# Order of two pieces in each slot of TensorE's queue: attention piece ahead of the hgrn2 level

## The chip, the cores and the metric

The kernel runs on one core of one Trainium2 chip. The metric is the device time of one execution in microseconds (us); lower is better. The time given for the kernel before is the median of 3 runs.

## What is computed

The program is a network of one dense block and two further layers over 256 tokens of width 1024. In each of the two layers (called layer 0 and layer 1 here, `l` in the code) the normed tokens `h` are projected once and the result feeds two token mixers, a gate for each, and then a mixture of experts:

```python
proj = h @ w_in
hq, hf, hi, hgate, cq, ckv, kr, gates = jnp.split(proj, IN_SPLITS, axis=-1)
o_a = hgrn2_mix(...)                      # 4 heads of 128, chunks of 64 tokens
o_a = rmsnorm(o_a, ...) * silu(hgate)
y_a = o_a @ w_br_a
y_b = mla_mix(cq, ckv, kr, pos, ...) @ w_br_b
g = sigmoid(gates)
merged = g_a * y_a + g_b * y_b
return merged @ w_out
```

`hgrn2_mix` is a linear recurrence with a decay per channel. Within a chunk it needs attention-like products of q and k, weighted by exp of differences of a running sum. `mla_mix` is a latent attention of 8 heads: q and k of 96 numbers per head (64 plain, 32 rotated), scores with a mask by chunks, a softmax, and the product with v of 64 numbers per head.

## The kernel before

Each engine has a queue of its own, written out by hand; semaphores join them. Weights come through a ring of 6 tiles of 1 MB in SBUF (`RING = 6`). The DMA of a tile (queue of SyncE, L432) waits until the tile six places earlier has been used by TensorE (`tiles_used`).

The products that must be exact to float32 are made of three: each such weight tile is split by ScalarE into a high part (`split` in its queue, L632, two halves) and by VectorE into the rest (`split` in its queue, L1808, two halves, event `mix_lo`).

The change is in the stretch that both layers have behind the projections: eight slots n = 0 to 7. TensorE does in slot n of the kernel before:

1. `by_token(gates{n})` (L1075): 48 matmuls of 256 columns for a tile of the gates, into bank n % 3. From slot 2 on it waits for the split of its tile, which ScalarE and VectorE make in their slot n - 2; from slot 3 on for the read of the bank (`gates`).
2. In layer 0 alone: three `ada` tiles (L1333, 48 matmuls of 32 rows by 256 columns), the modulation of layer 1.
3. The hgrn2 level n (L1579): 8 matmuls of 128 by 128 (16 passes in the trace) into banks 4 and 5. It waits for `hy` (written by VectorE in its slot n - 1) and `level_added`; its end is the event `level`.
4. `mla(n)`: a piece of the latent attention into banks 6 and 7. Slots 0 and 1 turn q, slots 2 and 3 turn k (`mla_turn`, L1519), slots 4, 5 and 6 make scores (`mla_scores` 0, 1 and 2, L1527), slot 7 turns the first block's probabilities (L1559). Slots 1 to 4 wait for ScalarE's copy of the turned piece before (`qT_out`, `kT_out`), slots 5 and 6 for the row maxima of the scores before (`mla_max`), slot 7 for `mla_max` and `mla_p`.

Behind the eight slots stand level 8 (L1588, waits for the eighth `hy`), the turns of the second block's probabilities (L1533), the hgrn2 output (L1597 to L1600) and the attention's output (L1614, L1616).

VectorE does in slot n: the span of level n + 1 (L2276, L2280, or L2288 to L2292; event `scans`), then it takes level n from its banks (`add_level`: L2303 in slot 0, L2305 in the others; it waits for `level`), multiplies the decays into `hy` (L2324, L2325; waits for `decay`), splits a gates tile (slots 0 to 5), in slots 4 to 6 masks the scores (L2334 or L2340; waits for `mla_s`) and takes their maximum (L1992, L1993; event `mla_max`), and in slots 5 to 7 scales the probabilities of the piece before (L2349, L2351; event `mla_p`).

ScalarE does in slot n: tanh of the gates (L948), the two exps of the decays (L959, L960; it waits for `scans` and for `hy` of VectorE's slot n - 1), its split of a gates tile (slots 0 to 5; in layer 0 it waits for the tile's DMA), then the copy of the turned q or k (L966, L972) in slots 0 to 3, or the exps of the scores (L979; waits for `mla_max`) in slots 4 to 6.

Of the kernel before, what the change touches and what calls it, by code (L numbers as in the profile page):

```python
# [67 lines left out]
def build(nc, a):  # L68

    ctx = ExitStack()  # L70
    with ctx:
# [293 lines left out]
        def slot_view(pos, kind):  # L365
            w = ring[:, pos % RING, :]
            if kind == 3 * QL:
                return w[:, 0:3 * QL].rearrange("p (k n) -> p k n", k=3)
            if kind in (512, 1024):
                return w.rearrange("p (k n) -> p k n", n=kind)  # L370
            return w[:, 0:KC * kind].rearrange("p (k n) -> p k n", k=KC)
# [43 lines left out]
        def _(sp):  # L415
# [18 lines left out]
            for entry in stream:  # L434
# [4 lines left out]
                if len(entry) == 4:  # L439
                    _, gate, up, down = entry  # L440
                    half = lambda w, e, kh: w[:, e, 4 * kh:4 * kh + 4, :]
                    down_half = lambda e, kh: down[:, e, 2 * kh:2 * kh + 2, :]
                    load(pos + 0, half(up, 0, 0))
                    load(pos + 1, half(gate, 0, 0))
                    load(pos + 2, half(gate, 0, 1))
                    load(pos + 3, half(up, 0, 1))
                    with sp.Fori(0, NE - 1) as i:
                        load(pos + 4, half(up, i + 1, 0), i)
                        load(pos + 5, down_half(i, 0), i)
                        load(pos + 6, down_half(i, 1), i)  # L450
                        load(pos + 7, half(gate, i + 1, 0), i)
                        load(pos + 8, half(gate, i + 1, 1), i)
                        load(pos + 9, half(up, i + 1, 1), i)
                    load(pos + 6 * NE - 2, down_half(NE - 1, 0))
                    load(pos + 6 * NE - 1, down_half(NE - 1, 1))
                    continue
                _, n, gate, up, down = entry

                def step(i, c, first=False):
# [565 lines left out]
        def _(pe):  # L1025
            mm, tr = pe.matmul, pe.transpose

            def landed(pos, i=0):
                pe.wait_ge(ring_full[pos % RING], 16 * i + 16 * (pos // RING + 1))
# [38 lines left out]
            def by_token(name, out, x_lo):  # L1068

                w = mix_parts(name)  # L1070
                h_parts = (hT_hi, x_lo)
                for t in range(T):
                    for k in range(KC):
                        for m, (hp, wp) in enumerate(PARTS):
                            ins = mm(out[:, t * FB:(t + 1) * FB], h_parts[hp][:, k, t * P:(t + 1) * P], w[wp][:, k, :],  # L1075
                                     start=k == 0 and m == 0, stop=k == KC - 1 and m == 2)
                ins.then_inc(tiles_used, 1)
# [247 lines left out]
            def ada(l, m, out):  # L1325

                pos = place[f"ada{m}.{l}"]
                landed(pos)
                w = slot_view(pos, FB)
                row, half = m // 2, m % 2  # L1330
                for k in range(KC):
                    g = 32 * (k % 4)
                    ins = mm(out[g:g + 32, half * FB:(half + 1) * FB], cpick[:, 12 + 32 * k - row:44 + 32 * k - row], w[:, k, :],  # L1333
                             start=m == 0 and k < 4, stop=m >= ADA_SLABS - 2 and k >= 4, skip_group_check=True)
                ins.then_inc(tiles_used, 1)
# [140 lines left out]
            for l in range(LAYERS):  # L1476
# [39 lines left out]
                def mla_turn(half, src, event):  # L1516
                    for h in range(4 * half, 4 * half + 4):
                        for t in range(T):
                            ins = tr(T_BANK[h % 4 // 2][0:DQK, (h % 2) * SEQ + t * P:(h % 2) * SEQ + (t + 1) * P],  # L1519
                                     src[:, t, h, :], ident[:, :])  # L1520
                    ins.then_inc(s[event], 1)

                def mla_scores(part):
                    for h in (range(MH), range(4), range(4, MH))[part]:
                        t, keys = (1, SEQ) if part else (0, P)
                        at = (h % 4 if part else h) * keys
                        ins = mm(T_BANK[at // 512][:, at % 512:at % 512 + keys], qT96[0:DQK, h, t * P:(t + 1) * P],  # L1527
                                 kT96[h // 4][0:DQK, h % 4, 0:keys], start=True, stop=True)
                    ins.then_inc(s["mla_s"], 1)
# [7 lines left out]
                def mla(n):  # L1537

                    if n < 2:
                        if n:  # L1540
                            pe.wait_ge(s["qT_out"], 2 * l + 1)
                        mla_turn(n, q96, "mla_qT")
                    elif n < 4:
                        if n == 2:
                            pe.wait_ge(s["qT_out"], 2 * l + 2)
                        else:
                            pe.wait_ge(s["kT_out"], 2 * l + 1)
                        mla_turn(n - 2, k96, "mla_kT")
                    elif n < 7:
                        if n == 4:  # L1550
                            pe.wait_ge(s["kT_out"], 2 * l + 2)
                        else:
                            pe.wait_ge(s["mla_max"], 3 * l + n - 4)
                        mla_scores(n - 4)
                    else:
                        pe.wait_ge(s["mla_max"], 3 * l + 3)
                        pe.wait_ge(s["mla_p"], 3 * l + 1)
                        for h in range(MH):
                            ins = tr(T_BANK[h // 4][:, (h % 4) * P:(h % 4 + 1) * P], p_first[:, h, :], ident[:, :])  # L1559
                        ins.then_inc(s["mla_pT"], 1)  # L1560

                for n in range(8):
                    if n >= 3:
                        pe.wait_ge(s["gates"], 8 * l + n - 2)
                    by_token(f"gates{n}.{l}", bank[n % 3], hT_lo_l)
                    if l == 0:
                        for m in range(ADA_EACH[1] * n, ADA_EACH[1] * (n + 1)):
                            ada(1, m, bank[3])
                    if n == 0:
                        pe.wait_ge(s["hk"], run)  # L1570
                        pe.wait_ge(s["hq"], run)
                        left, right = hk, hq
                    else:
                        pe.wait_ge(s["hy"], 8 * l + n)
                        pe.wait_ge(s["level_added"], 9 * l + n)
                        left = right = hy[:, :].rearrange("p (h s) -> p h s", h=HGH)
                    for t in range(T):
                        for h in range(HGH):
                            ins = mm(bank[4 + t][:, h * P:(h + 1) * P], left[:, h, t * P:(t + 1) * P],  # L1579
                                     right[:, h, t * P:(t + 1) * P], start=True, stop=True)  # L1580
                    ins.then_inc(s["level"], 1)
                    mla(n)

                pe.wait_ge(s["hy"], 8 * l + 8)
                pe.wait_ge(s["level_added"], 9 * l + 8)
# [946 lines left out]
```

## Time and profile before

| what | us |
|---|---|
| median of 3 runs | 1886.56 (1885.85 to 1888.33) |
| time of the profiled execution | 1887.39 |
| its span, first to last instruction | 1885.7 |
| TensorE busy | 1693.9 (90%) |
| VectorE busy | 1184.9 (63%) |
| ScalarE busy | 975.0 (52%) |
| mean granted TensorE clock | 0.948 of full speed |
| eight slots of layer 0, first gates matmul to level 8 | 686.25 to 788.02 |
| eight slots of layer 1, first gates matmul to level 8 | 1347.92 to 1421.71 |

TensorE has the largest busy share; the page's share is an average over stages with different limits, so the stretch of the slots is read by itself. The time outside the span is 1.7 us.

### The profile page before, as it was taken

How to read it: one execution, taken by the hardware profiler on the slowest of the kernel's cores; microseconds unless marked ns; L12 is line 12 of the kernel's file. 1: busy time of each engine (PE TensorE's matmuls, PEld its weight loads, DVE VectorE, ACT ScalarE, POOL GpSimd, SP SyncE). 2: the span in 40 equal slices, each digit the busy share in tenths (PEclk: the TensorE clock that was granted, in tenths of full speed). 3: DMA queues.
4: the chain of work that ended last, by engine and by line, in shares of the span. 5: the costliest groups of instructions: out<-in, count | busy, mean ns of one | idle time of the engine just before them, and what ended most of it. 6: DMA issues, size and time to landing. Idle time of an engine off the chain costs nothing.

```text
span 1885.7 us, 26698 instructions
## 1 busy us (share of the span) xinstructions
PE 1693.9 (90%) x10028; PEld 1408.3 (75%) x10028; DVE 1184.9 (63%) x1669; ACT 975.0 (52%) x1365; POOL 26.7 (1%) x58
## 2 busy tenths in 40 slices
PE   6999897899996989886899999979898769999995
PEld 6999785499995968743688888869695357888884
DVE  5544355554447444723788888854574378888886
ACT  4444344154434423401788888744341049888883
POOL 2000000000000000001000000000000010000000
PEclk9999998999998989998799999989899969999998
DMA  8555478845552559722398998935332308898992
GB/s 255 191 188 178 154 244 279 272 156 190 178 190 88 169 169 348 267 89 89 113 335 314 333 329 319 331 110 166 125 112 89 112 32 297 316 332 325 324 335 76
DMA packets 245831, 401.83 MB, mean 213 GB/s; under 512 B 6522, under 2 KB 151596, under 8 KB 245756
## 3 DMA queue, kind: packets, MB, share of 16 engines
q1 hardware_dynamic: 244792, 398.77, 61.6%
q0 software_dynamic: 592, 0.93, 0.2%
q10 hardware_dynamic: 372, 1.07, 0.2%
q8 instruction: 54, 0.88, 0.2%
q14 instruction: 21, 0.17, 0.0%
HBM read 399.70 MB, written 1.05 MB: 213 GB/s over the span
## 4 chain that ended last, share of the span: by engine, by line
PE 82%; DVE 10%; ACT 4%; issue 2%; DMA 1%; ACTq 0%; DVEq 0%
PE bank L1226 19%; PE bank L1168 14%; PE bank L1250 9%; PE bank L1097 8%; PE bank L1075 8%; PE bank L1181 6%; PE bank L1063 4%; PE bank L1262 3%; PE bank L1333 2%; DMA sb_ring<-in_w_in 1%; PE bank L1508 1%; PE bank L1086 1%; PE bank L1579 1%; DVE sb_w_lo L1808 1%; DVE sb_w_lo L1873 1%
## 5 line engine op out<-in xcount | busy, mean ns | idle before, releaser
L1873 DVE TENSOR_TENSOR sb_w_lo<-sb_ring,sb_moe_hi 128x1024 fp32r<-128x1024 f32 x384 | 448.4, 1220 | 29.5 <-ACT sb_moe_hi L697 29.2
L697 ACT ACTIVATE sb_moe_hi<-sb_ring 128x1024 fp32r<-128x1024 f32 x384 | 381.5, 1056 | 69.8 <-PE bank L1250 33.7
L1829 DVE TENSOR_TENSOR sb_w_lo<-sb_ring,sb_w_hi 128x1024 fp32r<-128x1024 f32 x128 | 151.1, 1222 | 172.1 <-ACT sb_w_hi L652 172.1
L1168 PE MATMUL bank<-sb_hT_hi,sb_w_hi 128*128 128x256 f32 x704 | 200.6, 285 | 3.6 <-DVE sb_hT_lo L1785 3.6
L652 ACT ACTIVATE sb_w_hi<-sb_ring 128x1024 fp32r<-128x1024 f32 x128 | 128.4, 1051 | 144.6 <-PE bank L1168 131.1
L1168 PE MATMUL bank<-sb_hT_hi,sb_w_lo 128*128 128x256 f32 x704 | 200.4, 285 | 0.0
L1168 PE MATMUL bank<-sb_hT_lo,sb_w_hi 128*128 128x256 f32 x704 | 200.4, 285 | 0.0
L1226 PE MATMUL bank<-sb_moe_hi,sb_xw_hi 128*128 128x512 f32 x480 | 193.6, 403 | 0.0
L1226 PE MATMUL bank<-sb_w_lo,sb_xw_hi 128*128 128x512 f32 x480 | 190.9, 398 | 0.0
L1226 PE MATMUL bank<-sb_moe_hi,sb_xw_lo 128*128 128x512 f32 x480 | 190.2, 396 | 0.0
L1250 PE MATMUL bank<-sb_moe_hi,sb_hid_hi 128*128 128x512 f32 x512 | 145.4, 396 | 2.9 <-DVE sb_hid_hi L1899 2.9
L1808 DVE TENSOR_TENSOR sb_w_lo<-sb_ring,sb_proj_hi 128x1024 fp32r<-128x1024 f32 x76 | 89.5, 1221 | 92.1 <-ACT sb_proj_hi L632 92.0
L1168 PEld LDWEIGHTS bank<-sb_hT_hi,sb_w_hi 128*128 128x128 f32 x704 | 136.4, 194 | 4.6 <-DVE sb_w_lo L1817 3.9
L1168 PEld LDWEIGHTS bank<-sb_hT_lo,sb_w_hi 128*128 128x128 f32 x704 | 136.4, 194 | 0.7
L1168 PEld LDWEIGHTS bank<-sb_hT_hi,sb_w_lo 128*128 128x128 f32 x704 | 136.3, 194 | 0.0
L1075 PE MATMUL bank<-sb_w_lo,sb_hT_hi 128*128 128x256 f32 x480 | 136.1, 284 | 0.0
L632 ACT ACTIVATE sb_proj_hi<-sb_ring 128x1024 fp32r<-128x1024 f32 x76 | 76.4, 1056 | 105.6 <-PE bank L1063 43.2
L1075 PE MATMUL bank<-sb_proj_hi,sb_hT_hi 128*128 128x256 f32 x416 | 120.0, 289 | 4.8 <-ACT sb_arena L942 4.8
L1075 PE MATMUL bank<-sb_proj_hi,sb_hT_lo_l 128*128 128x256 f32 x416 | 117.9, 283 | 0.0
L1250 PEld LDWEIGHTS bank<-sb_moe_hi,sb_hid_hi 128*128 128x128 f32 x512 | 93.8, 188 | 21.4 <-DVE sb_hid_hi L1899 3.4
L1226 PEld LDWEIGHTS bank<-sb_moe_hi,sb_xw_lo 128*128 128x128 f32 x480 | 91.3, 190 | 21.6
L1226 PEld LDWEIGHTS bank<-sb_w_lo,sb_xw_hi 128*128 128x128 f32 x480 | 91.4, 190 | 20.0
(465 smaller groups left out, 3132.9 us busy)
## 6 DMA issues: line engine op xcount, KB each, us to landing
sb_ring<-in_w_up SPq DMA_DIRECT2D x64, 1024.0 KB, 5.3
sb_ring<-in_w_gate SPq DMA_DIRECT2D x64, 1024.0 KB, 5.3
sb_ring<-in_w_down SPq DMA_DIRECT2D x64, 1024.0 KB, 4.8
sb_ring<-in_ada_w SPq DMA_DIRECT2D x48, 1024.0 KB, 7.7
sb_ring<-in_w_in SPq DMA_DIRECT2D x46, 1024.0 KB, 5.3
sb_ring<-in_ffn_w_in SPq DMA_DIRECT2D x44, 1024.0 KB, 5.0
sb_ring<-in_ffn_w_out SPq DMA_DIRECT2D x22, 1024.0 KB, 4.9
sb_ring<-in_w_out SPq DMA_DIRECT2D x12, 1024.0 KB, 5.0
```

Of the source, the lines that this page charges most:

```text
L632: A(mix_hi(name)[:, c], ring[:, pos % RING, c], ACT.Copy).then_inc(s["mix_hi"], 1)
L652: A(w_hi[:, q % 2, c], ring[:, (pos0 + q) % RING, c], ACT.Copy).then_inc(s["w_hi"], 1)
L697: A(moe_hi[:, q % 3, c], ring[:, at % RING, c], ACT.Copy).then_inc(s["moe_hi"], 1)
L1075: ins = mm(out[:, t * FB:(t + 1) * FB], h_parts[hp][:, k, t * P:(t + 1) * P], w[wp][:, k, :], start=k == 0 and m == 0, stop=k == KC - 1 an ...
L1097: ins = mm(out[2 * t + half][:, :], lhs[:, kk, t * P:(t + 1) * P], w[:, kk, half * 512:(half + 1) * 512], start=start and kk == 0, stop=st ...
L1168: ins = mm(bank[4 + 2 * p + b][:, jj * SEQ:(jj + 1) * SEQ], w[wp][:, k, jj * P:(jj + 1) * P], h_parts[hp][:, k, :], start=k == 0 and m == ...
L1181: ins = mm(acc[2 * t + half][:, :], h, w[wp][:, kk, half * 512:(half + 1) * 512], start=start and kk == 0 and m == 0, stop=stop and kk == ...
L1226: ins = mm(out[:, :], x_parts[xp][:, 4 * kh + k, 0:P], w[wp][:, k, :], start=kh == 0 and k == 0 and m == 0, stop=kh == 1 and k == 3 and m ...
L1250: ins = mm(bank[6 + half][:, :], h[hp][:, 2 * kh + kk, :], w[wp][:, kk, half * 512:(half + 1) * 512], start=kh == 0 and kk == 0 and m == 0 ...
L1808: ins = tt(w_lo[:, pos % RING, c], ring[:, pos % RING, c], mix_hi(name)[:, c].bitcast(F32), ALU.subtract)
L1829: ins = tt(w_lo[:, slot, c], ring[:, slot, c], w_hi[:, q % 2, c].bitcast(F32), ALU.subtract)
L1873: ins = tt(w_lo[:, slot, c], ring[:, slot, c], moe_hi[:, q % 3, c].bitcast(F32), ALU.subtract)
```

## The change

In the loop over the slots the call of `mla(n)` moves from behind the level to ahead of it. Nothing is added or removed, and the queues of the other engines stay as they are, instruction for instruction.

```diff
                     if l == 0:
                         for m in range(ADA_EACH[1] * n, ADA_EACH[1] * (n + 1)):
                             ada(1, m, bank[3])
+                    mla(n)
                     if n == 0:
                         pe.wait_ge(s["hk"], run)
                         pe.wait_ge(s["hq"], run)
...
                             ins = mm(bank[4 + t][:, h * P:(h + 1) * P], left[:, h, t * P:(t + 1) * P],
                                      right[:, h, t * P:(t + 1) * P], start=True, stop=True)
                     ins.then_inc(s["level"], 1)
-                    mla(n)
```

On TensorE, layer 1, the end of slot 4 (L1579 the level, L1527 the scores of part 0) stood before as:

```order
L1579 MATMUL bank<-sb_arena 128x128 [waits level_added,hy]
L1579 MATMUL bank<-sb_arena 128x128 x7
L1527 MATMUL bank<-sb_small_a,sb_arena 128x128 [waits kT_out]
L1527 MATMUL bank<-sb_small_a,sb_arena 128x128 x3
L1527 MATMUL bank<-sb_small_b,sb_arena 128x128 x4
L1075 MATMUL bank<-sb_proj_hi,sb_hT_hi 128x256 [waits mix_lo,gates]
```

The same place stands now as follows (the level is L1580 in the changed file):

```order
L1527 MATMUL bank<-sb_small_a,sb_arena 128x128 [waits kT_out]
L1527 MATMUL bank<-sb_small_a,sb_arena 128x128 x3
L1527 MATMUL bank<-sb_small_b,sb_arena 128x128 x4
L1580 MATMUL bank<-sb_arena 128x128 [waits level_added,hy]
L1580 MATMUL bank<-sb_arena 128x128 x7
```

The eight score matmuls, with their wait, have moved ahead of the level; in slots 5 and 6 the wait that moves with them is that for `mla_max`.

On TensorE, layer 0, slot 5 with the ends of the `ada` matmuls (L1333) ahead of it, as a difference:

```order
 L1333 MATMUL bank<-sb_ring,sb_cpick 32x256 x24
-L1579 MATMUL bank<-sb_arena 128x128 x8
 L1527 MATMUL bank<-sb_small_a,sb_arena 128x256 x4
+L1580 MATMUL bank<-sb_arena 128x128 x8
 L1075 MATMUL bank<-sb_proj_hi,sb_hT_hi 128x256
```

The level now stands between the scores of part 1 and the next gates tile. The last slot of layer 0, with level 8 (L1588) behind it:

```order
 L1333 MATMUL bank<-sb_ring,sb_cpick 32x256 x24
-L1579 MATMUL bank<-sb_arena 128x128 x8
 L1559 MATMUL bank<-sb_ident,sb_arena 128x128 x8
+L1580 MATMUL bank<-sb_arena 128x128 x8
 L1588 MATMUL bank<-sb_arena 128x128 x4
 L1533 MATMUL bank<-sb_ident,sb_arena 128x128 x8
```

Level 7 now stands behind the eight turns of L1559 and directly ahead of level 8.

## Rows read from the trace of the kernel before

**Rows 1.** The page: span, and busy time of two engines.

```profile
span 1885.7 us, 26698 instructions
PE 1693.9 (90%) x10028; PEld 1408.3 (75%) x10028; DVE 1184.9 (63%) x1669; ACT 975.0 (52%) x1365; POOL 26.7 (1%) x58
```

**Rows 2.** Stretches of the slots: length, busy PE, PEld, DVE, ACT, POOL, clock, DMA.

```profile
690.00:790.00 100.00, 94.30 (x956) 81.25 (x955) 54.55 (x87) 37.33 (x79) 0.00 (x0) 0.98 1.00 327
1340.00:1440.00 100.00, 91.18 (x705) 83.84 (x704) 70.35 (x116) 45.59 (x95) 0.00 (x0) 0.98 0.32 106
```

**Rows 3.** Waits, 1345 to 1435 us: who waited for whom, us, times, longest.

```profile
DVE sb_arena L2305 <- PE bank L1579: 10.5, 5, 2.5
PE bank L1588 <- DVE sb_arena L2325: 3.1, 1, 3.1
```

**Rows 4.** Chain that ended last, layer 1: start us, us, what.

```profile
1356.60 5.75 PE bank L1075 x48
1362.35 1.79 PE bank L1579 x16
1364.14 0.87 PE bank L1519 x8
...
1387.59 1.80 PE bank L1579 x16
...
1396.93 0.18 DVE sb_stat L1993
...
1401.94 0.69 DVE sb_arena L2324
...
1408.00 0.17 DVE sb_stat L1993
...
1416.46 0.18 DVE sb_stat L1993
```

**Rows 5.** Timeline of DVE, layer 1: start, us, engine, line, [idle <- releaser].

```profile
1394.36 1.28 DVE L2334 TENSOR_TENSOR sb_arena<-bank,sb_mla_mask 128x512 f32<-128x512 f32 x2
...
1398.81 1.35 DVE L2305 COPY_PREDICATED sb_arena<-sb_level_mask,bank 128x512 f32<-128x512 int32 x2 [1.12 <-PE bank L1579]
...
1411.29 1.36 DVE L2305 COPY_PREDICATED sb_arena<-sb_level_mask,bank 128x512 f32<-128x512 int32 x2
...
1417.87 1.34 DVE L2305 COPY_PREDICATED sb_arena<-sb_level_mask,bank 128x512 f32<-128x512 int32 x2
...
1420.36 0.69 DVE L2324 TENSOR_TENSOR sb_arena<-sb_arena 128x512 f32<-128x512 f32 x1 [1.15 <-ACT sb_arena L960]
```

**Rows 6.** Timeline of ACT, layer 0: copy of the turned q.

```profile
706.55 1.06 ACT L966 ACTIVATE sb_arena<-bank 96x512 f32<-96x512 f32 x2
```

**Rows 7.** Timeline of PE, layer 0: slots 1 and 5, and level 8.

```profile
706.25 2.05 PE L1579 MATMUL bank<-sb_arena 128*128 128x128 f32 x16
...
754.29 2.05 PE L1579 MATMUL bank<-sb_arena 128*128 128x128 f32 x16
758.95 2.87 PE L1527 MATMUL bank<-sb_small_a,sb_arena 96*128 96x256 f32 x8 [2.60 <-DVE sb_stat L1993]
...
788.02 1.16 PE L1588 MATMUL bank<-sb_arena 128*128 128x128 f32 x8 [1.95 <-DVE sb_arena L2325]
```

**Rows 8.** Chain, layer 0: scores of part 2 (slot 6) and level 7.

```profile
773.00 1.73 PE bank L1527 x8
...
783.21 2.00 PE bank L1579 x16
```

**Rows 9.** Timeline of DVE, layer 0: level 7 taken from its banks.

```profile
785.30 1.34 DVE L2305 COPY_PREDICATED sb_arena<-sb_level_mask,bank 128x512 f32<-128x512 int32 x2 [4.63 <-PE bank L1579]
```

**Rows 10.** Clock behind the gap ahead of level 8, layer 1 (columns as rows 2).

```profile
1422.00:1425.50 3.50, 3.50 (x19) 3.50 (x19) 1.61 (x5) 0.31 (x1) 0.00 (x0) 0.51 0.00 0
```

**Rows 11.** Timeline of PE: L1635 behind equal gaps in layers 0 and 1.

```profile
832.99 1.09 PE L1635 MATMUL bank<-sb_ident,sb_arena 128*128 128x128 f32 x8 [2.71 <-DVE sb_arena L2394]
...
1466.43 1.95 PE L1635 MATMUL bank<-sb_ident,sb_arena 128*128 128x128 f32 x8 [2.71 <-DVE sb_arena L2394]
```

## Prediction

> **What bounds the kernel now.** The page comes first: TensorE is busy for 90% of the span and VectorE for 63% [rows 1]. The change touches only the eight slots of each layer, so I read those by windows. There TensorE is busy for 94% of the stretch in layer 0 and 91% in layer 1; the DMA engines are full in layer 0 and at a third in layer 1 [rows 2]. A reorder on a busy engine is free as long as nobody waits for the piece that comes later, so the next view is who waits for the level: VectorE (L2305) waits for L1579 five times in layer 1, 10.5 us in all, at most 2.5 us [rows 3]. These waits have different weight. The chain that ended last tells it. Through slots 0 to 3 of layer 1 it is all TensorE: gates 5.75, level 1.79, turn 0.87 us, slot after slot [rows 4]. From the level of slot 4, which starts at 1387.59, it leaves TensorE: VectorE and ScalarE carry it through L1993 at 1396.93, 1408.00 and 1416.46, until level 8 starts on TensorE at 1421.71 after an idle time of 3.1 us [rows 3, 4]. So from slot 4 on the level's end feeds the chain, and TensorE waits for that chain at its end. In layer 0 the DMA sets ScalarE's and VectorE's pace up to slot 5; then VectorE idles 4.63 us for level 7 [rows 9], and TensorE idles 1.95 us for what comes of it [rows 7]. Nobody waits for the scores or the turned pieces: in slot 4 of layer 1 VectorE comes to the scores at 1394.36 [rows 5], and they end at about 1387.59 + 1.80 + 1.73 = 1391.1 [rows 4, 8].
>
> **The change part by part.** The number of instructions does not change, nor what each costs: 8 turns are 0.87 us, 8 score heads 1.73, a level 1.79 in layer 1 and 2.0 in layer 0 [rows 4, 8]. What changes is that each level ends later by the length of the piece ahead of it, and that the piece's own wait now stands ahead of the level.
>
> Slots 0 to 3, layer 1: the level ends 0.87 us later. VectorE waits 2.35 us for each of levels 1 to 4 (10.5 less the 1.12 of slot 5, over four) [rows 3, 5], and what it makes next, `hy`, is not needed until the level of the next slot, a gates tile of 5.75 us later. The split that follows serves the gates tile two slots on. TensorE has no new wait: the total per slot stays 8.41. Cost 0; without that cover it would be 0.87 once.
>
> Slot 4, layer 1: scores 0 (1.73) now stand ahead of level 4. Level 4 ends at 1387.59 + 1.73 + 1.80 = 1391.12, not 1389.39. VectorE stood waiting there, so its chain starts 1.73 late, and the maximum of slot 4 (L1993) ends at 1398.83, not 1397.10.
>
> Slot 5, layer 1: the gates end at 1396.87 as before (1391.12 + 5.75). Before, the level went next and hid the wait for `mla_max`. Now TensorE idles until 1398.9, makes scores 1 until 1400.6 and level 5 until 1402.4. VectorE took level 5 at 1398.81 [rows 5]; now it does so at 1402.5, 3.7 late. It had spare time there, since `hy` waited for ScalarE until 1401.94 [rows 4]. ScalarE's part comes at 1401.94 + 1.73 = 1403.7, VectorE's own at 1402.5 + 1.35 = 1403.85. So `hy` is 1.9 late, and the second maximum ends at 1408.17 + 1.9 = 1410.07.
>
> Slot 6, layer 1: gates from 1402.4 to 1408.15, idle until 1410.1, scores 2 until 1411.8, level 6 until 1413.6. VectorE took level 6 without idle time at 1411.29 [rows 5]; now at 1413.7, 2.4 late. The third maximum ends at 1416.63 + 2.4 = 1419.05.
>
> Slot 7, layer 1: gates until 1419.35, L1559 until 1420.2, level 7 until 1422.0. VectorE takes it from 1422.1 to 1423.45, where it began at 1417.87 before. ScalarE's exps, behind the third maximum, come 2.4 late. So L2324 starts at about 1423.5, against 1420.36 [rows 5], and level 8 follows it: **+3.1 us** for layer 1.
>
> Layer 0, slots 0 to 4: slot 1 shows a new wait. TensorE reaches the piece at 706.25 [rows 7], but ScalarE's copy of the first turned q runs from 706.55 to 707.6 [rows 6]: 1.3 us idle, which the level hid. Such waits come back up to slot 4, as TensorE arrives 2 us ahead of each copy. They don't add up, because the copies stand at the pace of the DMA. TensorE is then one level, 1.98 us, behind its old place at each slot's end. Would later use of tiles starve the DMA? The engines are full, with tiles queued [rows 2]; a slip of 2 us in a cadence of 12 us for four tiles (levels 1 and 5 start 48.0 us apart [rows 7]) should stay inside that queue. Its cost is 0; were it not covered, it would be up to 2 us.
>
> Layer 0, slot 5: scores 1 start at 758.95 with or without the change, since their maximum hangs on VectorE's chain from the DMA. Before, level 5 (754.29 to 756.3) lay in the wait; 2.60 us idle were left [rows 7]. Now the whole wait is idle, and the level goes behind the scores: +1.98 on TensorE, and there is no later wait in slots 6 and 7 to take it back. In slot 7, L1559 adds its 0.87 ahead of the level. Level 7 ended at 783.21 + 2.00 [rows 8], and VectorE had long been waiting [rows 9]: it takes it 1.98 + 0.87 = 2.85 later, and level 8, which hangs on that alone, moves from 788.02 by **+2.85 us**.
>
> Sum of both layers: 3.1 + 2.85 = 5.95. Behind level 8 the same chain as before follows, on TensorE and VectorE, and nothing there waits for a transfer, so I give nothing back.
>
> One price is unsettled: TensorE's clock after a gap. After the 3.1 us gap ahead of level 8 of layer 1 [rows 3] the granted clock was 0.51 for 3.5 us, the 1.2 GHz level [rows 10]. The same code, L1635, behind a gap of 2.71 us in both layers, took 1.09 us in one and 1.95 in the other [rows 11]: a gap of this size costs sometimes 0 and sometimes some 0.9 to 1.7 (3.5 us at 0.51, if all of it is matmul). The change makes the gap before level 8 of layer 0 some 2.75 long instead of 1.95, and adds two of 1.9 to 2.0 in layer 1; the one of 1.95 was followed by 1.16 for L1588, so full speed [rows 7]. I charge half a drop of about 1 us: +0.5. At the other end, three drops would cost 5.1. The Trainium skill (TensorE: Matmul & The Clock Gate, part 1) says that an idle stretch halves the clock, and that the phase in which it is looked at varies from run to run; the rows on L1635 agree. By that rule the new gaps are a toss, and the sum would lie between the plain one and the one with all drops.
>
> Forecast: the profiled execution goes from 1887.39 (span 1885.7) to 1893.8 (span 1892.2), as 1.7 lie around the span. The median of before is 0.8 below its profiled time, so the median comes to 1886.56 + 5.95 + 0.5 = **1893.0**.
>
> **The rivals.**
> - *The order is neutral.* TensorE's work is the same, and 10.5 us of waiting for levels in layer 1 [rows 3] can swallow the delay. It does in slots 0 to 3. Against it: in slots 5, 6 and 7 VectorE idles 1.12 us, nothing and nothing before L2305 [rows 5]. It would give 1886.6. Chance 0.12.
> - *One layer alone pays.* If the DMA's pace, or a slack that I missed, takes back layer 0's part, 1886.6 + 3.1 = 1889.7 stays; with layer 1's part gone, 1889.4. For it: layer 0 runs at full DMA. Against it: VectorE's 4.63 us in slot 7 are for TensorE, not for a transfer [rows 9]. Chance 0.12.
> - *More clock drops.* Each of the longer gaps costs its 1.7: with two beside the sum 1886.6 + 5.95 + 3.4 = 1895.9, with three 1897.6. For it: rows 10. Against it: the gap of 1.95 that kept its speed. Chance 0.14.
> - *Faster: the attention pieces bind.* The scores reach VectorE earlier by a level, 1.79 or 2.0 us, in slots 4 to 6. If L2334 and L2340 waited for TensorE, each slot's chain would shorten by as much: at most 3 x 1.79 + 3 x 2.0 = 11.4, so 1875.2. It decides as soon as VectorE idles before L2334 for L1527. Against it: VectorE came to L2334 3.2 us after the scores of slot 4 and shows no idle time before it [rows 5]. Chance 0.03.
>
> **How the numbers follow.** The forecast as summed has 0.59. The range goes from one layer alone (1889.4) to the sum with between two and three drops (1896.6); neutral and faster, 0.15 together, lie outside, with a little at the top. About 0.2% (3.8 us, so 1890.3) is what a measurement can tell from no change. Slower beyond it: the forecast, the clock case and a share of the one-layer case, 0.76; same: neutral and the rest of one-layer, 0.20; faster 0.04.
>
> **What would show it.** In the new trace: TensorE idle before L1527 in slots 5 and 6 of layer 1, some 1.9 us each, for L1993; idle before L1519 in slots 1 to 4 of layer 0, for ScalarE's copies; level 8 some 76.9 us after the first gates matmul of layer 1 (73.8 before) and 104.6 in layer 0 (101.8 before); the experts as long as before. The prediction is wrong if VectorE's idle time in slots 5 to 7 does not move, if the DMA of layer 0 shows pauses that stretch the slots, or if the stretch behind level 8 gives the delay back.

## The result and the profile after

| | median us | range, runs |
|---|---|---|
| before | 1888.18 | 1885.85 to 1893.80, 7 |
| changed | 1900.64 | 1898.31 to 1907.47, 7 |

The changed kernel takes 1.0068 of the time of before, 95% interval 1.0054 to 1.0083: 12.8 us (10.2 to 15.7) slower. The forecast was 1893.0, the range ended at 1896.6. Later runs of the same kernel gave 1.0054 (1.0033 to 1.0075) and 1.0049 (1.0036 to 1.0062). Three executions far outside all others, one of the changed kernel (3014.90 us) and two of before (7167.72 and 2224.72), are left out everywhere.

The page of the changed kernel, against [rows 1]:

```profile
span 1898.3 us, 26698 instructions
PE 1699.3 (90%) x10028; PEld 1410.8 (74%) x10028; DVE 1185.8 (62%) x1669; ACT 974.7 (51%) x1365; POOL 26.7 (1%) x58
```

Instructions are the same; the span is 12.6 us longer and TensorE is busy for 5.4 us more, with the same matmuls.

The timeline of PE in layer 0 (start us, us, engine, line, op; idle time and who ended it), against [rows 7]. L1580 is the level, L1579 before:

```profile
706.09 1.08 PE L1519 MATMUL bank<-sb_ident,sb_arena 128*96 128x128 f32 x8 [1.39 <-ACT sb_arena L966]
707.00 1.95 PE L1580 MATMUL bank<-sb_arena 128*128 128x128 f32 x16
...
757.65 2.97 PE L1527 MATMUL bank<-sb_small_a,sb_arena 96*128 96x256 f32 x8 [2.72 <-DVE sb_stat L1993]
...
784.62 1.95 PE L1580 MATMUL bank<-sb_arena 128*128 128x128 f32 x16
789.39 2.07 PE L1588 MATMUL bank<-sb_arena 128*128 128x128 f32 x8 [2.82 <-DVE sb_arena L2325]
791.25 1.72 PE L1533 MATMUL bank<-sb_ident,sb_arena 128*128 128x128 f32 x8
```

The slots started at 684.71 here (686.25 before), so level 8 comes 104.68 us after them, where it was 101.77. The wait for ScalarE's copy is there (1.39, and 0.82 and 0.84 in slots 2 and 3; none in slot 4, where one was forecast), the wait for the maximum stands alone (2.72), and the gap ahead of level 8 grew from 1.95 to 2.82. Behind that gap L1588 and L1533 took 2.07 and 1.72 us; before, L1588 took 1.16 behind its shorter gap [rows 7]. The windows view (columns as in rows 2) has the granted clock there at 0.52 and then at 1.00:

```profile
789.40:792.80 3.40, 3.40 (x16) 3.40 (x17) 1.85 (x6) 0.00 (x0) 0.00 (x0) 0.52 1.02 406
792.80:796.00 3.20, 3.20 (x32) 3.20 (x30) 0.31 (x1) 2.37 (x3) 0.00 (x0) 1.00 0.03 10
```

PE in layer 1, slots started at 1353.16 (1347.92 before):

```profile
1404.18 2.00 PE L1527 MATMUL bank<-sb_small_a,sb_arena 96*128 96x256 f32 x8 [2.02 <-DVE sb_stat L1993]
1406.02 1.95 PE L1580 MATMUL bank<-sb_arena 128*128 128x128 f32 x16
1415.77 2.34 PE L1527 MATMUL bank<-sb_small_b,sb_arena 96*128 96x256 f32 x8 [2.06 <-DVE sb_stat L1993]
1417.90 3.29 PE L1580 MATMUL bank<-sb_arena 128*128 128x128 f32 x16
...
1427.65 1.95 PE L1580 MATMUL bank<-sb_arena 128*128 128x128 f32 x16
1432.43 1.16 PE L1588 MATMUL bank<-sb_arena 128*128 128x128 f32 x8 [2.83 <-DVE sb_arena L2325]
```

Level 8 comes after 79.27 us, against 73.79. The two new waits are 2.02 and 2.06 long. Behind the first the next pieces ran at full clock (level 5: 1.95); behind the second they did not (level 6: 3.29). VectorE's timeline shows the releaser turned round: it idles for each of levels 5, 6 and 7, where it idled 1.12 us, none and none [rows 5]:

```profile
1408.07 1.39 DVE L2305 COPY_PREDICATED sb_arena<-sb_level_mask,bank 128x512 f32<-128x512 int32 x2 [3.35 <-PE bank L1580]
...
1421.30 1.37 DVE L2305 COPY_PREDICATED sb_arena<-sb_level_mask,bank 128x512 f32<-128x512 int32 x2 [2.38 <-PE bank L1580]
...
1429.70 1.34 DVE L2305 COPY_PREDICATED sb_arena<-sb_level_mask,bank 128x512 f32<-128x512 int32 x2 [1.80 <-PE bank L1580]
```

### The profile page after: what moved, and what is told of

It is laid out like the page before. It is cut to its first block, busy times and chain, and to the rows that moved or that the text cites. A ratio compares the mean times of both kernels' runs of the same rounds, so it can differ in the third digit from the quotient of the medians.

```text
span 1898.3 us, 26698 instructions
## 1 busy us (share of the span) xinstructions
PE 1699.3 (90%) x10028; PEld 1410.8 (74%) x10028; DVE 1185.8 (62%) x1669; ACT 974.7 (51%) x1365; POOL 26.7 (1%) x58
## 4 chain that ended last, share of the span: by engine, by line
PE 83%; DVE 10%; ACT 3%; issue 2%; DMA 2%; ACTq 0%; DVEq 0%
PE bank L1226 19%; PE bank L1168 13%; PE bank L1250 9%; PE bank L1097 8%; PE bank L1075 8%; PE bank L1181 6%; PE bank L1063 4%; PE bank L1262 3%; DMA sb_ring<-in_w_in 2%; PE bank L1333 1%; PE bank L1580 1%; PE bank L1508 1%; DVE sb_w_lo L1808 1%; DVE sb_w_lo L1873 1%; PE bank L1038 1%
```

## Where the time stands, stage by stage

Differences of start times, read from the timelines of the traces. "Slots": first gates matmul to level 8. "To br": level 8 to the attention's first output product (L1097). "Behind": first L1635 to the last expert's scatter (L1262), where no kernel here was edited.

| us | before | before again | changed | changed again |
|---|---|---|---|---|
| slots, layer 0 | 101.77 | 101.78 | 104.68 | 105.02 |
| to br, layer 0 | 13.68 | 13.69 | 15.07 | 15.28 |
| behind, layer 0 | 401.91 | 402.07 | 403.97 | 403.42 |
| slots, layer 1 | 73.79 | 73.78 | 79.27 | 79.27 |
| to br, layer 1 | 13.41 | 13.42 | 11.94 | 11.94 |
| behind, layer 1 | 399.95 | 399.95 | 403.02 | 403.02 |

The first two rows of a layer give 4.3 us in layer 0 and 4.0 in layer 1. The stages behind give 2.1 and 3.1 us more, though their code is the same. What is between the layers and at the end adds 0.8, and ahead of layer 0's slots the changed trace is 1.5 us shorter (684.71 against 686.25), also without an edit. Together that is the trace's 12.6 within 0.1.

The windows view over the whole stage behind layer 1, before and then changed, has equally many matmuls that are busy for 2.8 us longer, of the 3.1 us that the stage grew (in layer 0: 1.8 of 2.1):

```profile
1466.43:1866.38 399.95, 369.64 (x1597) 291.32 (x1597) 308.25 (x383) 278.98 (x367) 6.30 (x6) 0.95 0.69 250
```

```profile
1475.69:1878.72 403.03, 372.43 (x1597) 292.27 (x1597) 308.22 (x383) 278.73 (x367) 6.30 (x6) 0.94 0.68 248
```

So the difference is mostly the clock. L1349 (four passes of 512 columns ahead of the output product) shows it in layer 1, behind like gaps; before:

```profile
1471.78 1.95 PE L1349 MATMUL bank<-sb_arena,sb_ones 128*128 128x512 f32 x4 [1.34 <-ACT sb_hT L1004]
```

and changed:

```profile
1481.24 3.75 PE L1349 MATMUL bank<-sb_arena,sb_ones 128*128 128x512 f32 x4 [1.13 <-issue]
```

Windows over this stretch, before and then changed, have a granted clock of 0.82 and 0.50:

```profile
1466.40:1475.80 9.40, 7.53 (x26) 4.77 (x27) 6.24 (x10) 1.21 (x4) 0.00 (x0) 0.82 0.20 76
```

```profile
1475.70:1485.00 9.30, 7.68 (x21) 4.84 (x22) 4.90 (x8) 1.21 (x4) 0.00 (x0) 0.50 0.20 78
```

## The experiments

A "drop" is a stretch in which TensorE works at the lower granted clock. Theory after the result: the later levels cost what was forecast, in slots 4 to 7, and the rest is TensorE's clock, dropping at the new gaps or behind. Rivals: any move costs; or something outside the slots and outside the clock.

All kernels are summed up here. The ratio is to the runs of before on the same chip. Mean time is over a kernel's executions and stands against 1889.9 us, the mean of 110 runs of before; the clock is the mean granted one (before: 0.9469). "Slots" is slots and "to br" of both layers in the trace, against the first trace of before; "behind 0" and "behind 1" are the stages behind the two layers (before: 401.9 and 402.1, 399.95 both times). The last three kernels of the table and the changed kernel's last 5 runs were timed beside 18 runs of before with a mean of 1890.9; against these their means are 1.0 lower.

| kernel | ratio (95%) | mean, us | clock | slots | behind 0 | behind 1 |
|---|---|---|---|---|---|---|
| changed, 18 runs | see above | +11.4 | 0.9445 | +8.3 | 404.0, 403.4 | 403.0, 403.0 |
| e1_layer1 | 1.0019 (1.0007 to 1.0031) | +4.4 | 0.9468 | +8.1 | 404.0 | 403.0 |
| e2_layer0 | 1.0040 (1.0024 to 1.0056) | +7.3 | 0.9454 | +4.3 | 403.9 | 403.0 |
| e3_slots0to3 | 1.0020 (1.0009 to 1.0031) | +3.5 | 0.9455 | +0.8 | 404.1 | 403.2 |
| e4_slots4to7 | 1.0063 (1.0047 to 1.0078) | +11.7 | 0.9437 | +8.1 | 404.0 | 403.0 |
| b_same | 0.9988 (0.9974 to 1.0002) | -1.2 | 0.9473 | 0.0 | 402.1 | 399.95 |
| f1_fill | 1.0037 (1.0024 to 1.0050) | +7.1 | 0.9471 | +4.2 | 403.1 | 403.9 |
| v1_mid | 0.9999 (0.9985 to 1.0012) | +1.2 | 0.9449 | +0.9 | 401.8 | 402.9 |
| e5_slot4 | 0.9997 (0.9982 to 1.0013) | 0.0 | 0.9471 | +1.2 | 401.6 | 402.9 |
| e6_slots56 | 1.0029 (1.0011 to 1.0047) | +4.2 | 0.9427 | +3.9 | 401.6 | 399.95 |
| e7_slot7 | 1.0026 (1.0011 to 1.0040) | +4.8 | 0.9442 | +1.7 | 403.9 | 403.0 |
| v2_level7 | 1.0003 (0.9991 to 1.0015) | -0.3 | 0.9457 | -1.5 | 403.0 | 403.0 |
| d_delay | 1.0030 (1.0019 to 1.0040) | +6.7 | 0.9471 | +6.7, 6.5 of it added | 402.2 | 403.2 |
| f4_slots56 | 1.0039 (1.0025 to 1.0052) | +9.0 | 0.9457 | +5.5 | 403.3 | 403.1 |
| f3_level8 | 1.0039 (1.0027 to 1.0052) | +8.2 | 0.9463 | +7.6 | 401.9 | 402.9 |

**One layer or one group of slots.** The move is made conditional, for instance:

```diff
+                    if l == 1:
+                        mla(n)
                     if n == 0:
...
-                    mla(n)
+                    if not (l == 1):
+                        mla(n)
```

> The attention piece stands ahead of the level in layer 1 alone. Late-level theory: layer 1's slots grow by 3 to 4 us, layer 0's by nothing, so +3.5 us over the kernel before. Late level with clock: the new gaps of 2.0 us in slots 5 and 6 drop the clock in part of the executions, +5 to +7. Rival, a cost that sits outside the slots: +3.5 in the slots and some +3 more behind them, in the same places in every trace.

Layer 1's slots took 79.28 us, as in the changed kernel. The mean is +4.4 (2.5 to 6.3). The slots column's 8.1 holds 4.1 of layer 0, which was not edited: there level 8 stood 104.34 us after the start and "to br" took 15.17, as the clock dropped for longer in slot 5 (L1527 3.78 us) and again behind the gap of 1.96 us ahead of level 8 (L1588 2.06, L1533 1.83). So even an unedited layer 0 is this much longer in some execution; the traced one was the slowest of 12 (1900.96; six of them lay between 1890.7 and 1892.2). One trace of a kernel is therefore a sample, and may be far from its mean.

> The attention piece stands ahead of the level in layer 0 alone. Late-level theory: the first gates matmul to level 8 of layer 0 grows by 2.9 us, layer 1 by nothing: +2.9 us. With clock: the gap ahead of level 8 of layer 0 (1.95 before, 2.8 now) adds up to 1.7, +3 to +5. Rival (a cost outside the slots): more than +6.

Slots of layer 0: 104.65; those of layer 1: 73.78. The slots give 4.3, 2.9 of order and 1.4 of clock, but the mean is +7.3, more than the clock theory's upper end. Here the rival that puts cost outside the slots has its first support.

> The attention piece stands ahead of the level in slots 0 to 3 of both layers alone. Late-level theory: nothing in layer 1; in layer 0 the new waits for ScalarE's copies put TensorE 2 us behind at the end of slot 3, and the wait of slot 5 for the maximum (2.6 us) takes them back: 0, between -1 and +1. Rival (any move costs, since TensorE is busy): at least half of what the whole change costs, +6.

Layer 1's slots took 73.80, so nothing there; layer 0's took 102.56, with 1.52 us idle in one of the new waits for ScalarE's copies (slot 1, then 1.87 left in slot 5). The order costs 0.8, as forecast within a microsecond. The time is +3.5 (2.3 to 4.8), which was not forecast, and the two stages behind were 2.2 and 3.3 us longer than before.

> The attention piece stands ahead of the level in slots 4 to 7 of both layers alone. Late-level theory: all of the change's cost, +6.5 us without clock drops and up to +12 with them, the same as the whole change within 2 us. Rival (any move costs): half of it, +6.

+11.7, with layer 0's slots at 104.37 and layer 1's at 79.28: slots 4 to 7 alone cost as much as all eight. Parts do not add up: e3 and e4 make +15.2, against 11.4. "Any move costs half" falls.

> The attention piece stands ahead of the level in slot 4 of both layers alone. Late-level theory: layer 1's chain starts 1.75 us late and keeps it, layer 0's slot 5 takes it back: slots of layer 1 75.5, of layer 0 101.8, +1.75 us at full clock; the clock may add 0 to 4 to the time. Rival (the maxima's wait in slots 5 and 6 is what costs): 0.

Layer 1's slots: 75.96, 2.2 longer; 1.5 of that came back to br, where L1588 kept its full clock (1.16) behind a gap of 1.96, not 3.1. TensorE's clock was instead at 0.52 for 3.5 us from 1413.00 on, in slot 6, behind a wait of 1.55. In layer 0, where 101.8 was forecast, the slots took 100.84 and "to br" 15.15: slot 5's scores took 1.99 us behind a wait of 0.83 (2.87 before, [rows 7]), and L1588 (L1591 here) 1.73 behind the gap of 1.95 that had kept its clock before. So two drops of before came at other places. Slots and "to br" are 1.2 longer in this trace; the mean is 0.0 (-1.6 to 1.6), which excludes neither this 1.2 nor zero.

> The attention piece stands ahead of the level in slots 5 and 6 of both layers alone. Late-level theory: layer 0 +1.98 us (level 5 no longer lies in the wait for the maximum), layer 1 +0.8, so +2.8 at full clock, up to +7 with drops. Rival (slot 4 carries the cost): 0 to +1.

+4.2 (one of its 12 executions, 1903.27 us, had a mean clock of 0.902; without it the mean is +3.4 and the clock 0.9464). Layer 0's slots took 104.32 (the level no longer lies in the wait, and a longer drop), layer 1's 75.15 (+1.4, forecast 0.8). Slots 5 and 6 carry more than slot 4. The gap ahead of level 8 of layer 0 was 1.96 us, as before, and this time L1588 (L1591 here) took 1.83 behind it:

```profile
790.43 1.83 PE L1591 MATMUL bank<-sb_arena 128*128 128x128 f32 x8 [1.96 <-DVE sb_arena L2328]
```

> The attention piece stands ahead of the level in slot 7 of both layers alone. Late-level theory: layer 0 +0.87 us and layer 1 +0.5, so +1.3 at full clock; the gap ahead of level 8 of layer 0 grows from 1.95 to 2.8 and may drop the clock, up to +4 with that. Rival: 0.

Layer 0's slots 102.83 and layer 1's 74.47, so +1.1 and +0.7: the order's price is right. The mean is +4.8 (3.2 to 6.4), though, above the upper end that was expected, and the gap of 2.82 ahead of level 8 of layer 0 kept its clock (L1591 1.16). What is over does not lie in the slots of this trace; both stages behind are longer.

**Both kernels again.**

> The kernel before itself once more, for a second trace and for the granted clock of each run. Theory that part of the change's cost is a matter of where the clock's drops fall: its stages behind the slots differ by 1 to 2 us each from the first trace of before, without any edit, and its runs spread with their mean clock. Rival (the kernel before is the same each time): every stage agrees within 0.3 us with the first trace.

The stages behind agree with the first trace of before within 0.2 us; only ahead of the slots did single stages differ, by up to 1.4. The theory that the stages behind vary by themselves in each execution is not borne out by this pair. But both traced executions (1887.39 and 1887.61 us) lie below the mean of before, 1889.9, and none of its longer ones, up to 1897.4, was traced.

> The changed kernel itself once more. Both theories: +12 us within 3. Slots of layer 0 104.7 and of layer 1 79.3 us again if the drops inside the slots belong to the order; one of them shorter by 1.5 to 1.9 if they are a matter of the execution.

1901.9 us median, 1.0054. Its trace is of the execution of 3014.90 us and settles nothing.

> The changed kernel itself once more, since its second trace was a disturbed one. If the drops belong to the order, its stages repeat those of the first trace within 0.3 us: layer 0's slots 104.7, layer 1's 79.3, and the two stretches from the split of the merged rows to the end of the experts 404.0 and 403.0. If they are a matter of the execution, at least one of the four differs by 1.3 us or more.

Layer 1's slots and stage behind repeat to the hundredth. Layer 0's differ from the first trace by 0.34 us (slots) and 0.55 (behind): more than the 0.3 of the one expectation, less than the 1.3 of the other. Slot 6's drop is there again:

```profile
1415.15 2.38 PE L1527 MATMUL bank<-sb_small_b,sb_arena 96*128 96x256 f32 x8 [2.07 <-DVE sb_stat L1993]
1417.32 3.25 PE L1580 MATMUL bank<-sb_arena 128*128 128x128 f32 x16
```

So is the drop ahead of level 8 of layer 0 (L1588 2.08, L1533 1.55). The two new drops inside the slots thus repeat with the order in both traces. The second trace has one more in layer 0, behind the gap of 1.54 ahead of L1614, that the first lacks.

**Filling the gaps.** f1 keeps the changed order and gives TensorE work in its new gaps (the first edit computes the level once more without its event, the second turns the first block's probabilities into banks 0 and 2); f4 has only the first of these edits, f3 only the second:

```diff
+                    if (l == 0 and n == 5) or (l == 1 and n in (5, 6)):
+                        pe.wait_ge(s["hy"], 8 * l + n)
+                        pe.wait_ge(s["level_added"], 9 * l + n)
...
                     mla(n)
...
+                pe.wait_ge(s["gates"], 8 * l + 7)
+                for again in range(2):
+                    for h in range(MH):
+                        tr(P_BANK[h // 4][:, (h % 4) * P:(h % 4 + 1) * P], p_first[:, h, :], ident[:, :])
                 pe.wait_ge(s["hy"], 8 * l + 8)
```

> The changed kernel, with TensorE's new gaps filled: level 5 of both layers and level 6 of layer 1 are computed twice, once ahead of the attention piece's wait and once behind it, and ahead of level 8 sixteen turns of the first block's probabilities go into banks that are free. If the clock makes the cost beyond 6.7 us, the drops in the slots vanish and it ends 3 to 5 us below the changed kernel, +8 over before. If the later levels alone make it, filling changes nothing: +12, or more where the fill is longer than the gap.

With more work on TensorE the time fell from +11.4 to +7.1, by 4.3 (2.7 to 5.9), and the clock rose to 0.9471, that of before. PE of f1 in slot 6 of layer 1: the level computed twice (L1575 and L1588 here), 0.29 us idle between, and level 6 back at 1.95 where it took 3.29:

```profile
1410.11 1.95 PE L1575 MATMUL bank<-sb_arena 128*128 128x128 f32 x16
1412.35 1.99 PE L1527 MATMUL bank<-sb_small_b,sb_arena 96*128 96x256 f32 x8 [0.29 <-DVE sb_stat L2005]
1414.18 1.95 PE L1588 MATMUL bank<-sb_arena 128*128 128x128 f32 x16
```

and ahead of level 8 of layer 0 (L1595 the fill, L1600 level 8, L1533 at 1.04 where it took 1.72):

```profile
784.84 1.91 PE L1595 MATMUL bank<-sb_ident,sb_arena 128*128 128x128 f32 x16
787.85 1.16 PE L1600 MATMUL bank<-sb_arena 128*128 128x128 f32 x8 [1.10 <-DVE sb_arena L2337]
788.85 1.04 PE L1533 MATMUL bank<-sb_ident,sb_arena 128*128 128x128 f32 x8
```

This is the direct test of the clock's part: idle time was exchanged for useless work, in the same order, and 4.3 us came back. Not all of it is what the change had added. In slot 5 of layer 0 the filling also removed a drop that the kernel before has: L1527 took 1.99 us from 757.66 on, behind 0.71 of idle time, where it took 2.87 behind 2.60 [rows 7]. And the drop ahead of level 8 of layer 0 was not removed but came later, behind a gap of 1.54. The first line is before, the second f1; the clock of the next 3.4 us was 1.00 and 0.50:

```profile
796.16 0.40 PE L1614 MATMUL bank<-sb_small_a,sb_arena 128*64 128x128 f32 x2 [1.54 <-DVE sb_arena L2363]
```

```profile
796.00 0.66 PE L1626 MATMUL bank<-sb_small_a,sb_arena 128*64 128x128 f32 x2 [1.54 <-DVE sb_arena L2375]
```

> The changed kernel with only the gaps of slot 5 (both layers) and slot 6 (layer 1) filled by computing the level twice; the gap ahead of level 8 stays. If these gaps' drops carry the clock's part, most of what the full filling gave back (4.7 us of mean time) comes back here: +8 over before; if the gap ahead of level 8 does, +11.

+9.0. Layer 1's slots fell to 77.63, by 1.64, the price of slot 6's drop. But "to br" of layer 1 rose from 11.94 to 13.41: the gap of 2.83 ahead of level 8, which had kept its clock in the changed kernel, now lost it:

```profile
1430.31 2.00 PE L1596 MATMUL bank<-sb_arena 128*128 128x128 f32 x8 [2.83 <-DVE sb_arena L2333]
1432.10 1.90 PE L1533 MATMUL bank<-sb_ident,sb_arena 128*128 128x128 f32 x8
```

A drop removed at one gap came back at the next.

> The changed kernel with only the gap ahead of level 8 filled, by sixteen turns into free banks; the gaps of slots 5 and 6 stay. If that gap's drop in layer 0 carries the clock's part, +8 over before; if those of slots 5 and 6 do, +11.

+8.2. "To br" of layer 0 is back at 13.70, and the stage behind layer 0 is back at 401.9. Each filling alone gives back 2.4 (f4) or 3.2 (f3) of the 4.3 by the table, but only 1.3 and 2.1 against the changed kernel's 5 runs beside them, which is not clear of noise. So how the 4.3 is shared between the gaps is not shown.

**A delay without a gap.**

```diff
                 pe.wait_ge(s["ymT"], run)
                 pe.wait_ge(s["mod"], 2)
+                for again in range((26, 32)[l]):
+                    tr(bank[again % 4][:, 0:P], p_first[:, again % 8, :], ident[:, :])
```

> The kernel before, with nothing moved and TensorE busy for longer at one place of each layer: ahead of the attention's first output product it makes 26 (layer 0) and 32 (layer 1) turns of 0.11 us whose result is overwritten, 6.3 us in all. It delays what is behind as the changed order does (2.9 and 3.4 us) without a new gap. Theory that the gaps' own drops make the extra cost: +6.3. Theory that a shift of the stages behind is enough to bring them into their slower form: +6.3 and 2 to 5 more, with 46.9, 37.8 and 46.1, 37.6 us in the stages behind.

+6.7 in the mean (+5.7, 4.5 to 6.9, against the runs of before beside it) for 6.3 us of work, clock 0.9471. In its trace the stage behind layer 0 is as short as before (402.2), the one behind layer 1 longer (403.2, against 399.95). A delay alone therefore costs about its own length on average, and a longer stage behind layer 1 in the trace does not show in the mean.

**The other way round.** v1 puts the level ahead of the second half of the gates matmuls in slots 4 to 7; v2, shown here, puts only level 7 of layer 0 ahead of the slot's three `ada` tiles, which follow its event:

```diff
-                    if l == 0:
+                    last = l == 0 and n == 7
+                    if l == 0 and not last:
...
                     ins.then_inc(s["level"], 1)
+                    if last:
...
```

> The other way round: in slots 4 to 7 of both layers the level goes ahead of the second half of the gates matmuls, the attention piece stays behind them. If the end of the level feeds the chain, as the late-level theory has it, the slots of layer 1 shrink by about 1.7 us (VectorE waits 2.3 for level 4) and those of layer 0 by 1.95 (the gap ahead of level 8): -3.6 us against before. Rival (TensorE's work alone counts): 0.

No gain, where -3.6 was expected: the mean is +1.2, the slots took 102.29 in layer 0 and 74.41 in layer 1. In layer 1 the chain changed engines: `hy` now waits for ScalarE, whose tanh waits for gates that end a level later (VectorE's idle time ahead of L2324, L2331 in this file, in slot 4):

```profile
1392.13 0.69 DVE L2331 TENSOR_TENSOR sb_arena<-sb_arena 128x512 f32<-128x512 f32 x1 [2.67 <-ACT sb_arena L960]
```

In layer 0 the wait in slot 5 grew to 3.75 us.

> The kernel before, with one piece moved the other way: in slot 7 of layer 0 the level stands ahead of the three ada tiles. VectorE idles 4.63 us for that level before, so the slots of layer 0 shrink by 1.9 us and the gap ahead of level 8 (1.95) vanishes: -1.9 us at full clock. If the clock's drops behind it fall as in the trace of before, -2; if any shift of the stages behind costs as it did for the other orders, up to +3.

Level 8 of layer 0 follows L1559 without a gap:

```profile
783.14 1.09 PE L1559 MATMUL bank<-sb_ident,sb_arena 128*128 128x128 f32 x8
784.07 1.06 PE L1592 MATMUL bank<-sb_arena 128*128 128x128 f32 x8
```

The slots of layer 0 shrank by 1.7 us to 100.07 and the trace shows -1.5 to br, yet no gain in time is seen (-0.3, ratio 1.0003; a gain of 1.5 us is still inside the ratio's interval). In the trace the stages behind were 1.1 and 3.0 us longer than before. No version here beats the kernel before.

## Why the prediction was wrong

**What held.** The sign and the mechanism of the order's part: the level's end feeds the chain, and its lateness in slots 4 to 7 is what the order costs. Slots 0 to 3 cost nothing in layer 1 and 0.8 in layer 0; the DMA of layer 0 was not starved (its share from 690 to 790 us was 0.99, 1.00 before). Layer 0's term was 2.85 and measured 2.9 (3.3 in the second trace). So close a match is in part luck: alone, slots 4 to 7 gave 2.6 (e4) and slots 0 to 3 gave 0.8 (e3), where the sum had 2.85 and 0. The new waits were 1.39, 2.02 and 2.06 us where 1.3, 2.0 and 1.95 were forecast. The rivals "neutral" and "faster" fall.

**Layer 1's term** was 3.1. The slots took 5.5 longer; 1.64 of it is slot 6's clock drop, as f4 shows, so the order's share is 3.8, 0.7 more than the hand sum. Most of this can be read in the hand-over from TensorE to VectorE: the sum has 3.6 us from the start of the scores to VectorE's copy of the level (1398.9 to 1402.5 in slot 5), the trace 3.89 (1404.18 to 1408.07), and slots 5 and 6 both pass through it.

**The step that failed** is the clock's term: "I charge half a drop of about 1 us: +0.5", with nothing charged behind level 8, where "the experts as long as before" was a sign to look for. The mean says +11.4 us (10.0 to 12.8; against the runs of before beside them, the changed kernel's three sets of runs were 13.0, 12.0 and 9.3 slower). The order has 6.7 (2.9 + 3.8), so 4.7 is left, where 0.5 was charged. Filling the gaps gave back 4.3, and the mean granted clock went from 0.9445 to that of before. An estimate from all timed runs agrees: the rows show two levels, full and half, so a mean clock c over a time t means 2(1 - c)t at half, which is 201 us before and 211 changed; the 10 us more cost up to 5.2 if TensorE worked through all of them. Of the 4.7 the traces place 1.4 at the drop ahead of level 8 of layer 0 and 1.64 at slot 6 of layer 1, less 1.5 where layer 1's gap ahead of level 8, 2.83 and not 3.1, lost its drop: 1.5 net. I had taken the one gap of 1.95 that kept its clock as a sign that gaps of about 2 are free. The next gap of 2.06 was not, twice, and in e6 one of 1.96 was not either. The rows on L1635, which the prediction took to agree with a phase that varies from run to run, stand in one execution: they show that the length of a gap does not decide, not that runs differ.

**The rest, some 3 us,** seems to lie behind the slots, but this is argued and not shown. Take from each mean what its slots show. For the kernels with 401.6 to 402.2 behind layer 0 (b_same, v1, e5, e6, d_delay, f3) there remain -1.2 to +0.6; for those with 403.0 or more, 2.7 to 3.6 (changed, e2, e3, e4, e7, f1, f4), but 1.2 in v2, while e1, whose traced execution was its slowest, has -3.7 by this count. This sorting was made after the fact, from one trace of most kernels. And "behind 1" does not sort them at all: this stage was 2.9 to 3.9 us longer in every traced kernel but before and e6, also in v1, e5, d_delay and f3, whose means leave nothing over. The two traces of before were besides below its mean: 1887.4 and 1887.6 against 1889.9, so some 2.5 us of the traces' 12.6 is not the change's; that the longer executions of before have such a stage too would explain both, but none was traced. What decides the length of the stages behind stays open: it is not the delay alone (d_delay), it does not go with the length of the slots (e3 is 0.8 longer in its slots and has the longer stage behind layer 0, e6 3.9 longer and has the shorter one), and v2, faster in its slots, has the longer one too.

The case "more clock drops", 1895.9 to 1897.6 with a chance of 0.14, was the nearest, and too low as well, with 1900.64 measured. It counted drops at the new gaps only, and missed that a drop can also come at gaps that were there before, in the slots and behind them.

## What to carry to other kernels

A piece that others wait for should not go behind a piece nobody waits for; to move it further ahead gave nothing here (v1, v2). And a piece that lies in another's wait is free only there. With the wait moved in front of it, both are paid. Gaps of 1.5 to 3 us kept the clock in some traces here and lost it in others. So let the range reach one drop for each added gap, 1.4 to 1.7 us here, and a few microseconds more for stages that are not edited at all. To see the clock's share, fill the gap with useless matmuls in the same order: if the time falls, it was the clock, and the trace tells whether the drop went or only moved.

## What was not expected of the hardware

- More work made the kernel faster: f1 adds 3 levels and 32 turns on TensorE and takes 4.3 us less than the changed kernel.
- Gaps of 2.02 and 2.06 us, 11.6 us apart, kept and lost the full clock in the same trace, and a gap of 2.83 kept it in the changed kernel and lost it in f4. The length of a gap does not tell it. The Trainium skill (TensorE: Matmul & The Clock Gate, part 1) calls the phase run-variable. The timed runs agree (the mean clock of before's runs lies between 0.942 and 0.950, and e1's unedited layer 0 was slower in its trace); yet by two traces each of two kernels the stages behind the slots repeated within 0.6 us, most of them within 0.2.
- Runs of one kernel spread by some 10 us (before: 1885.4 to 1897.4), and the slower ones have the lower mean clock (e1: 1891.56 at 0.949, 1900.96 at 0.943).
